# Layer norms of a decoder trunk, run in two halves of the tokens between dense products

## The chip, the cores and the metric

One core of a Trainium2 chip runs the whole program once. The metric is the device time of one launch in microseconds (us).

## What is computed

The program is one inference step of a decoder trunk: 512 prompt tokens and 8 sample tokens (520 columns) of width 1024 go through two layers. Each layer is a mixer and a gated ConvFFN, and a layer norm follows each of the four sublayers. The products are the bulk of it. Cut to what matters here:

```python
ALPHA = (2 * DEPTH) ** 0.25
def layer_norm(x, g, b):
    mu = jnp.mean(xf, axis=-1, keepdims=True)
    var = jnp.mean(jnp.square(xf - mu), axis=-1, keepdims=True)
    return ((xf - mu) * lax.rsqrt(var + NORM_EPS) * g + b)
def run_trunk(...):
    for layer in range(DEPTH):
        h = mixer(x)                 # gla/retention in layer 0, short convolution in layer 1
        x = layer_norm(ALPHA * x + h, ln1_g[layer], ln1_b[layer])
        h = conv_ffn(x, ...)         # (silu(g) * a) @ w_out after x @ w_in and a width-3 convolution
        x = layer_norm(ALPHA * x + h, ln2_g[layer], ln2_b[layer])
```

## The kernel before

Activations lie with features on the partitions: x32 is 8 feature tiles (KD = 8) of 128 x 520. Every dense product is done with both operands split into a high and a low part (x_hi, x_lo, w_hi, w_lo), so one 128-feature step is three matmuls, and the 520 tokens are two halves of 256 and 264 columns (HALVES), one PSUM bank each. Weights come in units of 1024 x 256 (the FFN's output product: three units of 8, 8 and 6 feature steps for 256 outputs). A unit makes two output tiles, f = 0 and 1, in acc(0) and acc(1), and costs 96 matmuls (72 where it has 6 steps). For each unit SyncE loads w_raw, ScalarE copies it to w_hi (stage_hi, L317), VectorE subtracts to w_lo (stage_lo, L322); the next unit's w_hi waits until the unit two before it has been used.

There is no scheduler: every engine's order is written out by hand, and semaphores tie them. There are four layer norms, n = 0 to 3. Norm 0 follows the mixer's output product, norm 1 the first FFN's, norm 2 the short convolution's, and norm 3 ends the program. At each of norms 0 to 2 this happens. The last weight unit of the output product makes feature tiles 6 and 7. VectorE adds each finished tile to x32 (L1480) and to a running sum ln_s1 (L1487); ScalarE squares it (L1110); GpSimd adds the squares up in ln_s2 (L901). Then TensorE sums over the partitions: token_sums (L687) is five matmuls with a single column of ones, for ln_s2, ln_s1 and the last square. VectorE turns these into mean and variance (L1511 to L1517), ScalarE takes the root (L1131), and TensorE spreads mean and inverse deviation over the partitions (spread, L696). VectorE adds the mean (L1534) and multiplies by the inverse (L1538), tile by tile; ScalarE applies gain and bias (L1148) and copies to x_hi (L1149); GpSimd makes x_lo (L859). The next product's first unit (first_unit and k_step, L356 and L359) consumes x_hi and x_lo tile by tile as they come. These float32 matmuls of sums and spreads leave two records each in the trace. Tile 5's handling on VectorE has the sums of tiles 0 to 5 in it (L1489, L1487), followed by stage_lo of the next product's first unit.

After the first unit of an FFN, accumulator acc(0) is free again only when ScalarE (L1166, L1168) and then VectorE (L1554, L1555, L1558) have read it; the second unit begins in acc(0). After norm 1 the short convolution's product follows, and one ScalarE copy (L1196) frees acc(0).

## Time and profile before

| | us |
|---|---|
| median of 3 runs | 1405.11 |
| lowest, highest | 1399.22, 1409.91 |
| span of the profiled execution | 1409.5 |
| PE busy in it | 1362.5 (97%) |
| DVE, ACT, POOL busy | 711.2, 482.1, 113.4 |
| mean granted TensorE clock | 0.956 |

The span is the hardware profiler's time from the first to the last instruction of one execution. It lies 0.4 us under the highest of the three runs and 4.4 us above their median; no time apart from the span is given for the profiled execution. TensorE is busy 97% of the span, so the kernel ends when TensorE has worked through its list. A granted clock of 1.00 is 2.4 GHz, of 0.50 it is 1.2 GHz.

### The profile page before, as it was taken

What the parts mean: (1) busy time and instruction counts of PE and PEld (TensorE: products, weight loads), DVE (VectorE), ACT (ScalarE), POOL (GpSimd) and SP (SyncE); (2) the same over time, 40 slices, a digit from 0 to 9 for tenths busy, and PEclk for the clock granted to TensorE, in tenths of its full rate; (3) what the DMA queues carried; (4) which work ended last, traced back from release to release, by engine and by line L of the source; (5) the groups of instructions that cost most, each with busy time, mean ns of one, the idle gap of its engine ahead of it and who ended that gap; (6) DMA issues with size and microseconds to landing.
All of it is one profiled execution on the core that took longest, in us unless ns stands there. A gap on an engine that the chain in (4) does not pass through costs nothing.

```text
span 1409.5 us, 24966 instructions
## 1 busy us (share of the span) xinstructions
PE 1362.5 (97%) x10861; PEld 1336.9 (95%) x10861; DVE 711.2 (50%) x905; ACT 482.1 (34%) x640; POOL 113.4 (8%) x77
## 2 busy tenths in 40 slices
PE   7999999999999999999999899999999999999994
PEld 6899998899989999999999899999899999999994
DVE  2657832234666565654225443346656656552255
ACT  3433231132354343443122433323543434341232
POOL 3000003100230000000002300002300000000023
PEclk9999998698989999999999899999899999999996
DMA  7222212311212222223222122222123222233201
GB/s 252 84 69 90 64 61 82 120 46 47 74 61 89 90 89 89 90 89 112 83 90 83 61 90 89 90 90 92 61 73 106 88 91 89 89 98 119 97 23 61
DMA packets 123556, 121.91 MB, mean 86 GB/s; under 512 B 2481, under 2 KB 121164, under 8 KB 123476
## 3 DMA queue, kind: packets, MB, share of 16 engines
q1 hardware_dynamic: 112916, 115.32, 25.2%
q10 hardware_dynamic: 10432, 5.24, 1.3%
q8 instruction: 52, 0.85, 0.2%
q0 software_dynamic: 144, 0.39, 0.1%
q14 instruction: 12, 0.10, 0.0%
HBM read 114.79 MB, written 6.55 MB: 86 GB/s over the span
## 4 chain that ended last, share of the span: by engine, by line
PE 89%; DVE 4%; ACT 2%; SPq 1%; POOL 1%; DMA 1%; issue 1%; DVEq 0%; ACTq 0%; POOLq 0%
PE ps L344 26%; PE ps L346 25%; PE ps L345 25%; PE ps L687 2%; PE ps L542 2%; PE ps L356 1%; PE ps L696 1%; POOL x_lo L859 1%; ACT x L1148 1%; PE ps L675 1%; ACT x_hi L1149 1%; DMA w_raw<-in_w_mix_in 1%; PE ps L359 1%; DVE tmp L1487 1%; DVE y_tok L1526 1%; SPq L404 1%
## 5 line engine op out<-in xcount | busy, mean ns | idle before, releaser
L344 PE MATMUL ps<-x_hi,w_hi 128*128 128x256 f32 (+1 forms) x2144 | 616.9, 288 | 0.0
L346 PE MATMUL ps<-x_hi,w_lo 128*128 128x256 f32 (+1 forms) x2144 | 611.0, 285 | 0.0
L345 PE MATMUL ps<-x_lo,w_hi 128*128 128x256 f32 (+1 forms) x2144 | 609.2, 284 | 0.0
L344 PEld LDWEIGHTS ps<-x_hi,w_hi 128*128 128x128 f32 x2144 | 409.9, 191 | 2.7 <-issue 1.2
L345 PEld LDWEIGHTS ps<-x_lo,w_hi 128*128 128x128 f32 x2144 | 411.0, 192 | 0.1
L346 PEld LDWEIGHTS ps<-x_hi,w_lo 128*128 128x128 f32 x2144 | 409.9, 191 | 0.0
L322 DVE TENSOR_TENSOR w_lo<-w_raw,w_hi 128x2048 fp32r<-128x2048 f32 (+2 forms) x103 | 234.9, 2280 | 238.1 <-ACT w_hi L317 237.8
L317 ACT ACTIVATE w_hi<-w_raw 128x2048 fp32r<-128x2048 f32 (+2 forms) x103 | 192.6, 1870 | 188.1 <-PE ps L346 174.7
L344 PE MATMUL ps<-h_hi,w_hi 128*128 128x264 f32 (+1 forms) x896 | 254.7, 284 | 0.8 <-DVE x L1491 0.8
L346 PE MATMUL ps<-h_hi,w_lo 128*128 128x264 f32 (+1 forms) x896 | 252.7, 282 | 0.0
L345 PE MATMUL ps<-h_lo,w_hi 128*128 128x264 f32 (+1 forms) x896 | 252.7, 282 | 0.0
L344 PEld LDWEIGHTS ps<-h_hi,w_hi 128*128 128x128 f32 x896 | 168.3, 188 | 1.1 <-DVE w_lo L322 1.0
L346 PEld LDWEIGHTS ps<-h_hi,w_lo 128*128 128x128 f32 x896 | 168.8, 188 | 0.0
L345 PEld LDWEIGHTS ps<-h_lo,w_hi 128*128 128x128 f32 x896 | 168.7, 188 | 0.1
L1166 ACT ACTIVATE tmp<-ps,vecs 128x520 f32<-128x520 f32 x88 | 69.2, 786 | 174.6 <-PE ps L346 166.3
L901 POOL TENSOR_TENSOR tmp<-tmp 128x520 f32<-128x520 f32 x24 | 34.4, 1435 | 1010.8 <-ACT tmp L1110 1009.8
L1554 DVE TENSOR_TENSOR tmp<-tmp,past_ffn 128x8 f32<-128x8 f32 x88 | 15.2, 173 | 128.9 <-ACT last_rows L1168 128.9
L1558 DVE SCALAR_TENSOR_TENSOR tmp<-ps,vecs,tmp 128x510 f32<-128x510 f32 x88 | 65.9, 749 | 11.2 <-DVE tmp L1555 1.5
L1555 DVE SCALAR_TENSOR_TENSOR tmp<-ps,vecs,tmp 128x511 f32<-128x511 f32 x88 | 65.9, 749 | 0.0
L1173 ACT ACTIVATE tmp<-tmp 128x520 f32<-128x520 f32 x44 | 28.1, 639 | 84.2 <-DVE tmp L1558 84.2
L859 POOL TENSOR_TENSOR x_lo<-x,x_hi 128x520 fp32r<-128x520 f32 x32 | 47.9, 1511 | 45.3 <-ACT x_hi L1149 34.2
L1565 DVE TENSOR_TENSOR h_lo<-tmp,h_hi 128x520 f32 (+1 forms) x44 | 30.8, 700 | 40.1 <-ACT h_hi L1175 40.1
(233 smaller groups left out, 1124.6 us busy)
## 6 DMA issues: line engine op xcount, KB each, us to landing
w_raw<-in_w_ffn_in SPq DMA_DIRECT2D x44, 1024.0 KB, 4.9
w_raw<-in_w_ffn_out SPq DMA_DIRECT2D x16, 1024.0 KB, 5.0
w_raw<-in_w_mix_in SPq DMA_DIRECT2D x14, 1024.0 KB, 5.1
w_raw<-in_w_sc_in SPq DMA_DIRECT2D x12, 1024.0 KB, 4.9
w_raw<-in_w_ffn_out SPq DMA_DIRECT2D x8, 768.0 KB, 4.5
w_raw<-in_w_mix_out SPq DMA_DIRECT2D x4, 1024.0 KB, 5.1
w_raw<-in_w_sc_out SPq DMA_DIRECT2D x4, 1024.0 KB, 5.2
x_tok<-in_x_prompt SPq DMA_DIRECT2D x2, 1024.0 KB, 7.6
```

The costliest lines, as they stand in the source:

```text
L317: e.activation(w_hi[:, par, 0:k, 0:c], w_raw[:, par, 0:k, 0:c], ACT.Copy).then_inc(hi_made, 1)
L322: e.tensor_tensor(w_lo[:, par, 0:k, 0:c], w_raw[:, par, 0:k, 0:c], w_hi[:, par, 0:k, 0:c].bitcast(F32), ALU.subtract).then_inc(lo_made, 1)
L344: e.matmul(out, wh, xh[:, k, lo:hi], start=(first and i == 0), stop=False)
L345: e.matmul(out, wh, xl[:, k, lo:hi], start=False, stop=False)
L346: mm = e.matmul(out, wl, xh[:, k, lo:hi], start=False, stop=(last and i == len(ks) - 1))
L542: mm = e.matmul(bank(4 + h, P, c * C, C), k[p, h // 2, t], q[p, h // 2, t], start=True, stop=True)
L859: e.tensor_tensor(x_lo[:, f, :], x32[:, f, :], x_hi[:, f, :].bitcast(F32), ALU.subtract).then_inc(sem("x_made"), 1)
L901: e.tensor_tensor(ln_s2, ln_sq[:, 0, :] if t == 1 else ln_s2, ln_sq[:, t % 4, :], ALU.add).then_inc(sem("ln_added"), 1)
L1166: e.activation(tmp[:, 2 * s + f, :], acc(f), ACT.Identity, bias=ffn_vec(l, 3, tile), scale=ffn_vec(l, 2, tile))
L1555: e.scalar_tensor_tensor(t[:, 1:T], acc(f)[:, 0:T - 1], ffn_vec(l, 1, tile), t[:, 1:T], ALU.mult, ALU.add).then_inc(sem("tap_done"), 1)
L1558: e.scalar_tensor_tensor(t[:, 2:T], acc(f)[:, 0:T - 2], ffn_vec(l, 0, tile), t[:, 2:T], ALU.mult, ALU.add).then_inc(acc_free, 1)
L1565: e.tensor_tensor(h_lo[:, bass.ds(2 * i + f, 1), :], tmp[:, 6 + f:7 + f, :], h_hi[:, bass.ds(2 * i + f, 1), :].bitcast(F32), ALU.subtract) ...
```

## The change

Norms 0, 1 and 2 are worked in the two halves of the tokens. The last unit of the output product (closing_unit) does both tiles of tokens 0 to 255 first, then both tiles of tokens 256 to 519. The sums of the first half of the tokens stand in the middle of its third quarter, the two spreads of that half in its fourth quarter. The first unit of the next product (opening_unit) does tokens 0 to 255 of all 8 feature steps first, with the second half's sums ahead of step 2, and its spreads ahead of steps 4 and 5; then it does tokens 256 to 519. VectorE, ScalarE and GpSimd do the adds, squares, shifts, scalings and splits in halves too, in a new order. The gain goes from ScalarE into VectorE's scaling. Norm 3 keeps its order. The core of the diff:

```diff
+        TOKEN_TILES = [(0, 1), (2, 3, 4)]
+        TILES, ADDED = KD + 2, KD - 1
...
-            def token_sums(out, squares, start=True, stop=True):
-                for j in range(5):
+            def token_sums(out, squares, start=True, stop=True, js=range(5)):
+                for j in js:
...
             def ln_sums(n):
...
-                e.wait_ge(sem("ln_mean_made"), n + 1)
-                spread(2, ln_inv[:, 1, :]).then_inc(sem("ln_spread"), 1)
-                e.wait_ge(sem("ln_inverse"), n + 1)
-                spread(3, ln_inv[:, 0, :]).then_inc(sem("ln_spread"), 1)
...
+            def half_sums(n, half):
+
+                js = TOKEN_TILES[half]
+                e.wait_ge(sem("ln_added"), ADDED * n + 6 + half)
+                token_sums(bank(7, P, 0, 5), ln_s2, True, False, js)
+                e.wait_ge(sem("ln_totaled"), TILES * n + 8 + 2 * half)
+                token_sums(bank(5, P, 0, 5), ln_s1, js=js).then_inc(sem("ln_var"), 1)
+                e.wait_ge(sem("ln_squared"), TILES * n + 8 + 2 * half)
+                token_sums(bank(7, P, 0, 5), ln_sq[:, (KD - 1) % 4, :], False, js=js).then_inc(sem("ln_var"), 1)
+
+            def half_mean(n, half):
+                e.wait_ge(sem("ln_mean_made"), 2 * n + half + 1)
+                spread(2, ln_inv[:, 1, :], TOKEN_TILES[half]).then_inc(sem("ln_spread"), 1)
+
+            def half_scale(n, half):
+                e.wait_ge(sem("ln_inverse"), 2 * n + half + 1)
+                spread(3, ln_inv[:, 0, :], TOKEN_TILES[half]).then_inc(sem("ln_spread"), 1)
...
+            def closing_unit(n, pr, u, k0, ks, only, xh, xl):
+
+
+                e.wait_ge(lo_made, u + 1)
+                for half in range(2):
+                    for f in range(2):
+                        if only and not half:
+                            e.wait_ge(acc_free, 2 * pr + f - 1)
+                        for i in range(ks):
+                            if half and f == 0 and i == ks // 2:
+                                half_sums(n, 0)
+                            if half and f == 1 and i == 0:
+                                half_mean(n, 0)
+                            if half and f == 1 and i == 2:
+                                half_scale(n, 0)
+                            mm = half_k(u % 2, i, f, k0 + i, half, xh, xl, only and i == 0, i == ks - 1)
...
+            def opening_unit(n, u, pr):
+
+
+                made = KD + 2 * KD * n
+                e.wait_ge(lo_made, u + 1)
+                e.wait_ge(sem("ln_centered"), TILES * n + 8)
+                for half in range(2):
+                    if half:
+                        e.wait_ge(acc_free, 2 * pr)
+                    both = [(k, f) for k in range(KD if half == 0 else KD // 2) for f in range(2)]
+                    apart = [(k, f) for f in range(2) for k in range(KD // 2, KD)] if half else []
+                    for k, f in both + apart:
+                        if half == 0 and f == 0:
+                            if k == 2:
+                                half_sums(n, 1)
+                            if k == 4:
+                                half_mean(n, 1)
+                            if k == 5:
+                                half_scale(n, 1)
+                        lo, hi = HALVES[half]
+                        wh, wl = (w[:, u % 2, k, f * P:(f + 1) * P] for w in (w_hi, w_lo))
+                        e.wait_ge(sem("x_hi_made"), made + KD * half + k + 1)
+                        e.matmul(acc_half(f, half), wh, x_hi[:, k, lo:hi], start=(k == 0), stop=False)
+                        e.matmul(acc_half(f, half), wl, x_hi[:, k, lo:hi], start=False, stop=False)
+                        e.wait_ge(sem("x_made"), made + KD * half + k + 1)
+                        mm = e.matmul(acc_half(f, half), wh, x_lo[:, k, lo:hi], start=False, stop=(k == KD - 1))
...
+                for half, (lo, hi) in enumerate(HALVES):
+                    e.wait_ge(sem("ln_squared"), TILES * n + 7 + 2 * half)
+                    e.tensor_tensor(ln_s2[:, lo:hi], ln_s2[:, lo:hi], ln_sq[:, 2, lo:hi], ALU.add).then_inc(sem("ln_added"), 1)
+                for half, (lo, hi) in enumerate(HALVES):
+                    for f in range(KD):
+                        split_x(f, KD + 2 * KD * n + KD * half + f + 1, lo, hi)
...
+                def half_x(f, half):
+                    lo, hi = HALVES[half]
+                    e.wait_ge(sem("ln_scaled"), 2 * KD * n + KD * half + f + 1)
+                    link(e.activation(x32[:, f, lo:hi], x32[:, f, lo:hi], ACT.Identity, bias=vec(g, col_b + f)))
+                    e.activation(x_hi[:, f, lo:hi], x32[:, f, lo:hi], ACT.Copy).then_inc(sem("x_hi_made"), 1)
...
+                half_square(6, 0)
+                half_square(7, 0)
+                half_root(0)
+                half_square(6, 1)
                 for f in range(KD):
-                    e.wait_ge(sem("ln_scaled"), KD * n + f + 1)
-                    link(e.activation(x32[:, f, :], x32[:, f, :], ACT.Identity, bias=vec(g, col_b + f), scale=vec(g, col_g + f)))
-                    e.activation(x_hi[:, f, :], x32[:, f, :], ACT.Copy).then_inc(sem("x_hi_made"), 1)
+                    if f == 2:
+                        half_square(7, 1)
+                    half_x(f, 0)
+                half_root(1)
+                stage_hi(e, u + 4 * per + 1)
+                for f in range(KD):
+                    half_x(f, 1)
...
                     for g in range(per):
                         stage_lo(e, u + per * j + g + 1)
+                    if j == 3 and n < 2 * DEPTH - 1:
+                        break
...
+                def scaled(half):
+                    lo, hi = HALVES[half]
+                    made = 2 * KD * n + KD * half
+                    for f in range(KD + 2):
+                        if half == 0 and f == 4:
+                            closing(1, 1)
+                        if f < KD:
+                            e.wait_ge(sem("ln_spread"), 4 * n + 2 * half + 1)
+                            e.tensor_tensor(x32[:, f, lo:hi], x32[:, f, lo:hi], acc_half(2, half), ALU.add).then_inc(sem("ln_shifted"), 1)
+                        if f >= 2:
+                            e.wait_ge(sem("ln_spread"), 4 * n + 2 * half + 2)
+                            e.wait_ge(sem("ln_shifted"), made + f - 1)
+                            e.scalar_tensor_tensor(x32[:, f - 2, lo:hi], x32[:, f - 2, lo:hi], vec(V_LN, col_g + f - 2), acc_half(3, half),
+                                                   ALU.mult, ALU.mult).then_inc(sem("ln_scaled"), 1)
+
+                closing(0, 0)
+                closing(1, 0)
+                moments(0)
+                closing(0, 1)
+                scaled(0)
+                moments(1)
+                scaled(1)
+                stage_lo(e, NEXT[n] + 1)
```

TensorE at norm 0 before, from the last dense products of the output product to the first of the FFN (ones,tmp are the token sums, ident,ln_inv the spreads):

```order
L344 MATMUL ps<-h_hi,w_hi 128x264
L345 MATMUL ps<-h_lo,w_hi 128x264
L346 MATMUL ps<-h_hi,w_lo 128x264
L687 MATMUL ps<-ones,tmp 128x1 x15
L696 MATMUL ps<-ident,ln_inv 128x128 x4
L696 MATMUL ps<-ident,ln_inv 128x8
L696 MATMUL ps<-ident,ln_inv 128x128 x4
L696 MATMUL ps<-ident,ln_inv 128x8
L356 MATMUL ps<-x_hi,w_hi 128x256
L356 MATMUL ps<-x_hi,w_hi 128x264
```

TensorE at norm 0 now: the first half's sums inside the closing unit, whose dense products go on behind them:

```order
L803 MATMUL ps<-h_hi,w_hi 128x264
L804 MATMUL ps<-h_hi,w_lo 128x264
L805 MATMUL ps<-h_lo,w_hi 128x264
L689 MATMUL ps<-ones,tmp 128x1 x6
L803 MATMUL ps<-h_hi,w_hi 128x264
L804 MATMUL ps<-h_hi,w_lo 128x264
L805 MATMUL ps<-h_lo,w_hi 128x264
```

and the second half's sums, ahead of feature step 2 of the opening unit:

```order
L850 MATMUL ps<-x_hi,w_hi 128x256
L851 MATMUL ps<-x_hi,w_lo 128x256
L853 MATMUL ps<-x_lo,w_hi 128x256
L689 MATMUL ps<-ones,tmp 128x1 x9
L850 MATMUL ps<-x_hi,w_hi 128x256
L851 MATMUL ps<-x_hi,w_lo 128x256
L853 MATMUL ps<-x_lo,w_hi 128x256
```

Where 15 sums and two whole spreads stood in one block between two products, there are now blocks of 6 and 9 sums, and dense products stand behind each.

VectorE at norm 0 before, from the running sums of tiles 0 to 5 (tmp) over stage_lo (w_lo) to tiles 6 and 7 and the mean:

```order
L1489 COPY tmp<-x_49 128x520
L1487 TENSOR_TENSOR tmp<-tmp,x_49 128x520 x5
L322 TENSOR_TENSOR w_lo<-w_raw,w_hi 128x2048
L1480 TENSOR_TENSOR x_49<-x_49,ps 128x520
L1482 MEMSET ones_one 128x1
L1487 TENSOR_TENSOR tmp<-tmp,x_49 128x520
L1480 TENSOR_TENSOR x_49<-x_49,ps 128x520
L1482 MEMSET ones_one 128x1
L1487 TENSOR_TENSOR tmp<-tmp,x_49 128x520
L1511 TENSOR_SCALAR ln_inv<-ps 128x5
```

and now, the same stretch:

```order
L1594 COPY tmp<-x_49 128x520
L1592 TENSOR_TENSOR tmp<-tmp,x_49 128x520 x5
L324 TENSOR_TENSOR w_lo<-w_raw,w_hi 128x2048
L1621 TENSOR_TENSOR x_49<-x_49,ps 128x256
L1626 TENSOR_TENSOR tmp<-tmp,x_49 128x256
L1621 TENSOR_TENSOR x_49<-x_49,ps 128x256
L1626 TENSOR_TENSOR tmp<-tmp,x_49 128x256
L1632 TENSOR_SCALAR ln_inv<-ps 128x2
L1634 TENSOR_TENSOR ln_var<-ln_inv 128x2
L1636 SCALAR_TENSOR_TENSOR ln_var<-ps,ln_var 128x2
L1638 RECIPROCAL ln_inv<-ln_inv 128x2
L1621 TENSOR_TENSOR x_49<-x_49,ps 128x264
```

The running sums and stage_lo stand where they stood; behind them come four half operations, on which the first half's sums wait, and the first half's mean and inverse come before the second half of tile 6.

ScalarE at norm 1 before, from the last squares (tmp) over stage_hi of the next product's second unit (w_hi) and the root to the first outputs:

```order
L1110 ACTIVATE tmp<-x_49 128x520 x3
L317 ACTIVATE w_hi<-w_raw 128x2048
L1131 ACTIVATE ln_inv<-ln_var,eps 128x5
L1148 ACTIVATE x_49<-x_49,vecs 128x520
L1149 ACTIVATE x_hi<-x_49 128x520
L1148 ACTIVATE x_49<-x_49,vecs 128x520
L1149 ACTIVATE x_hi<-x_49 128x520
L1148 ACTIVATE x_49<-x_49,vecs 128x520
L1149 ACTIVATE x_hi<-x_49 128x520
```

and now, at the passage from the first half's outputs to the second half's:

```order
L1209 ACTIVATE x_49<-x_49,vecs 128x256
L1210 ACTIVATE x_hi<-x_49 128x256
L1209 ACTIVATE x_49<-x_49,vecs 128x256
L1210 ACTIVATE x_hi<-x_49 128x256
L1204 ACTIVATE ln_inv<-ln_var,eps 128x3
L319 ACTIVATE w_hi<-w_raw 128x2048
L1209 ACTIVATE x_49<-x_49,vecs 128x264
L1210 ACTIVATE x_hi<-x_49 128x264
L1209 ACTIVATE x_49<-x_49,vecs 128x264
L1210 ACTIVATE x_hi<-x_49 128x264
```

stage_hi of the second unit stood ahead of the root, and now stands behind the first half's outputs and ahead of the second half's; so it does at norms 0 and 2.

## Rows read from the trace of the kernel before

**Rows 1.** The page, part 1: busy us, share of the span, instructions.

```profile
PE 1362.5 (97%) x10861; PEld 1336.9 (95%) x10861; DVE 711.2 (50%) x905; ACT 482.1 (34%) x640; POOL 113.4 (8%) x77
```

**Rows 2.** Timeline of TensorE at norm 0: start, us, then idle before.

```profile
369.62 0.28 PE L344 MATMUL ps<-h_hi,w_hi 128*128 128x256 f32 x1
...
380.99 0.28 PE L346 MATMUL ps<-h_hi,w_lo 128*128 128x264 f32 x1
381.67 3.88 PE L687 MATMUL ps<-ones,tmp 128*128 128x1 f32 x30 [0.40 <-POOL tmp L901]
385.41 4.41 PE L696 MATMUL ps<-ident,ln_inv 128*128 128x128 f32 x20
392.23 0.77 PE L356 MATMUL ps<-x_hi,w_hi 128*128 128x256 f32 x2 [2.40 <-ACT x_hi L1149]
...
408.12 0.36 PE L344 MATMUL ps<-x_hi,w_hi 128*128 128x256 f32 x1
```

**Rows 3.** The same at norm 1.

```profile
769.67 0.28 PE L344 MATMUL ps<-h_hi,w_hi 128*128 128x256 f32 x1
...
778.17 0.28 PE L346 MATMUL ps<-h_hi,w_lo 128*128 128x264 f32 x1
...
790.26 0.48 PE L356 MATMUL ps<-x_hi,w_hi 128*128 128x256 f32 x2 [2.40 <-ACT x_hi L1149]
...
806.12 0.28 PE L344 MATMUL ps<-x_hi,w_hi 128*128 128x256 f32 x1
```

**Rows 4.** Windows at norms 0 and 1: us, PE busy (x), granted clock, DMA.

```profile
384.50:385.00 0.50, 0.50 (x6) 0.67 0.00 0
...
398.00:398.50 0.50, 0.50 (x4) 0.68 0.00 0
...
780.50:781.00 0.50, 0.50 (x5) 0.61 0.00 0
...
797.50:798.00 0.50, 0.50 (x6) 0.82 0.00 0
```

**Rows 5.** Chain that ended last, merged: sums and spreads amid dense work.

```profile
291.64 4.36 PE ps L687 x40
300.45 2.13 PE ps L696 x20
```

**Rows 6.** Timeline of VectorE at norm 0, then at norm 1.

```profile
376.61 2.28 DVE L322 TENSOR_TENSOR w_lo<-w_raw,w_hi 128x2048 fp32r<-128x2048 f32 x1
...
774.18 0.70 DVE L1480 TENSOR_TENSOR x<-x,ps 128x520 f32<-128x520 f32 x1
```

**Rows 7.** Timeline of ScalarE at norm 0.

```profile
382.58 1.89 ACT L317 ACTIVATE w_hi<-w_raw 128x2048 fp32r<-128x2048 f32 x1
...
390.60 0.82 ACT L1148 ACTIVATE x<-x,vecs 128x520 f32<-128x520 f32 x1 [4.44 <-DVE x L1538]
391.45 0.64 ACT L1149 ACTIVATE x_hi<-x 128x520 fp32r<-128x520 f32 x1
391.99 0.81 ACT L1148 ACTIVATE x<-x,vecs 128x520 f32<-128x520 f32 x1
...
405.47 0.79 ACT L1166 ACTIVATE tmp<-ps,vecs 128x520 f32<-128x520 f32 x1 [2.20 <-PE ps L359]
```

**Rows 8.** Timelines of VectorE and GpSimd at norm 0, where the two meet.

```profile
397.75 3.38 DVE L322 TENSOR_TENSOR w_lo<-w_raw,w_hi 128x2048 fp32r<-128x2048 f32 x1
...
399.07 3.23 POOL L859 TENSOR_TENSOR x_lo<-x,x_hi 128x520 fp32r<-128x520 f32 x1
...
402.26 1.30 POOL L859 TENSOR_TENSOR x_lo<-x,x_hi 128x520 fp32r<-128x520 f32 x1
```

**Rows 9.** Groups by line and form: shapes xcount, then busy us, mean ns.

```profile
L981 ACT ACTIVATE k_tok<-ps 128x256 f32<-128x256 f32 x4 | 1.2, 389 | 0.3 <-PE ps L557 0.3
L945 ACT ACTIVATE gate_t<-ps,vecs 128x520 f32<-128x520 f32 x2 | 1.3, 692 | 1.4 <-PE ps L524 1.4
...
L1399 DVE SCALAR_TENSOR_TENSOR samp<-samp,a_samp,ps 128x128 f32<-128x128 f32 x16 | 4.3, 340 | 4.0 <-PE ps L662 4.0
```

178 lines of the change are left out of this document (106 added, 72 removed).

## The prediction

> **What bounds the kernel now.** The page's busy times come first: TensorE is busy 97% of the span [rows 1], so the end moves only with TensorE's list, its waits and its clock. The timeline of TensorE at a norm shows what the change can reach [rows 2, 3]. At norm 0 the closing unit starts at 369.62 and its last dense product ends at 381.27 (380.99 + 0.28): 96 matmuls in 11.65 us, 0.121 each. The next product's second unit begins at 408.12. Between lie 26.85 us, of which the first unit's 96 matmuls need 11.65, so norm 0 costs 15.2 us. At norm 1 the same reading gives 806.12 - 778.45 = 27.7 and a cost of 16.0. Norm 2 repeats norm 0. Together 46.4 us.
>
> Three things are in it. First, work: 30 records of sums and 20 of spreads [rows 2]; amid dense work these took 4.36 / 40 = 0.109 and 2.13 / 20 = 0.107 us each [rows 5], so 3.3 + 2.1 = 5.4 us. Second, waiting: 2.40 us for the first x_hi [rows 2, 3], and small gaps. Third, the clock: it fell to the 1.2 GHz level in the window at 384.50, three us after the dense products stopped, and came back in the window at 398.00, six us after they resumed at 392.23; at norm 1 it fell in the window at 780.50 and returned in the one at 797.50 [rows 4, 2, 3].
>
> **The work stays, so at most 30 us can go.** Sums and spreads are the same in number (6 + 9 and 4 + 6 against 15 and 10). If nothing else were left, norms 0 and 2 would gain 15.2 - 5.4 = 9.8 each and norm 1 10.6: 30.2 us. What is left has to be followed along three engines.
>
> **Half operations.** The trace has few of 256 columns. On ScalarE a copy of 256 columns takes 0.39 from PSUM [rows 9], and a copy of 520 takes 0.64 from SBUF [rows 7]; I take 0.42 for the half copy (bounds 0.32, half of the long one, and 0.64), as the 0.39 row is the nearest. Identity with a bias alone takes 0.69 at 520 [rows 9] against 0.82 with bias and gain [rows 7]; half of it with the same fixed part, 0.52 (bounds 0.35 and 0.69). A half tile therefore costs ScalarE about 0.97 from scaled x to x_hi, and one follows another every 0.87. VectorE: 0.34 at 128 columns [rows 9] and 0.70 at 520 [rows 6] give 0.46 at 256 (bounds 0.35 and 0.70). GpSimd: 1.30 at 520 [rows 8]; half 0.65, and I take 0.70 (bounds 0.65 and 1.30).
>
> **Norm 0, closing unit.** TensorE reaches the first half's sums after 48 + 12 matmuls, at 369.62 + 7.3 = 376.9. They wait for tiles 6 and 7 of that half on VectorE. VectorE is not there: its running sums end at 376.61 and its stage_lo runs until 378.9 [rows 6], and both stand ahead of the half operations as before. Before, that lag was covered by the second tile's dense products, which ended at 381.27. Now four half operations (1.7 us, the pairs overlapping a little) end at 380.6, and **a new stall of 3.7 us** stands in the middle of the closing unit. Six sums follow (12 records, 1.3 us), then 36 dense matmuls (4.4) and four spreads (0.9; mean and inverse are ready by then, since the root's chain is under 1 us). At full clock the unit ends at 387.2.
>
> The clock won't stay full. From 376.9 to 381.9 no dense product runs, longer than the 2.1 to 3.4 us after which it fell in the two cases above, and it then took six us of work to return. I take half rate from 380.6 to about 388: 7.4 us in which half the work is done, a loss of 3.7, and the closing unit ends at 390.9. The Trainium skill (TensorE: Matmul & The Clock Gate, "HAM oscillation — how this bites in real kernels") says that short runs of matmuls broken by waits keep throwing the clock back, which speaks against this change; the trace agrees in the windows named.
>
> **Norm 0, opening unit.** Now ScalarE is the pace. VectorE adds the second half of tile 7 first (0.95, to 391.9), then shifts tile 4 and scales tile 2 (0.8, to 392.7). ScalarE makes tile 2 (393.7) and five more at 0.87 (398.0). Then come root (0.3) and the second unit's stage_hi (1.9 [rows 7]), which before was done at 384.5 under TensorE's sums and now stands between the halves: 400.2. The second half's tiles follow: 401.1 for the first, seven more at 0.88 for the last, 407.3. GpSimd's last split ends at 408.0, and tile f = 0 is complete at 408.1. The dense work, sums and spreads of the opening unit fit beneath this as long as the clock is full. The second unit can't start yet: acc(0) must be read first. Before, ScalarE began that at 405.47 [rows 7] and the second unit started at 408.12, 2.65 us later, just covered by f = 1's products. Now f = 1 has only 12 matmuls left behind f = 0 (1.45 us), so 1.2 us of it come into the open. Start at 410.8 against 408.12: **+2.7**.
>
> One more price. When stage_lo and GpSimd's split met, the first took 3.38 in place of 2.28 and the second 3.23 in place of 1.30 [rows 8, 6]: one waited for the other. Behind scaled(1) the second unit's stage_lo now meets the last splits of the second half. If GpSimd is held for 1.6 to 1.9 us there, the start becomes 412.4, or +4.3. The Trainium skill (SBUF — State Buffer, "SBUF: two separate sides") has a rule for it: a VectorE operation with two SBUF inputs and a GpSimd one that reads SBUF exclude each other for the whole instruction. By it the sum would be +4.3 for each such norm, without it +2.7; rows 8 agree with the rule.
>
> I take **+3.5 for norms 0 and 2 each**. The lower bound is the chain without the loss of clock, 2.7 - 3.7 = -1.0, the upper one +5.5 (the lock, and the clock falling once more at the second half's nine sums, 1.9 us of work in which no dense product runs).
>
> **Norm 1.** Here the output product has three units for a pair of tiles, and VectorE is free at 774.18 [rows 6]. TensorE gets to the sums after 36 + 9 matmuls, at 769.67 + 5.4 = 775.1; the half operations end at 775.9, a stall of 0.8. The closing unit ends at 781.4, tile 2 of x_hi is made at 784.1, the first half at 788.4, stage_hi at 790.6, the second half at 797.7, x_lo at 798.4. A ScalarE copy frees acc(0), so the second unit follows f = 1's products, at 800.0 against 806.12: -6.1. The meeting of stage_lo and GpSimd takes 1.8 back, one fall of the clock in the opening unit about as much again. I take **-2.5**; bounds -6.1 and +1.
>
> **The sum.** 2 x 3.5 - 2.5 = +4.5 us. Against the profiled span it gives 1409.5 + 4.5 = 1414.0. That span lies 4.4 above the median of the three runs, so I add the term to the median: 1405.1 + 4.5 = **1409.6**. With all lower bounds it is -8.1 (1397), with all upper ones +12 (1417). The rest of the program is untouched.
>
> **Rivals.** *The halves hide the norm (faster by over 1%).* If VectorE got through tile 6 and 7 in time and the clock never fell, the 30.2 us above would go: 1375. It counts as faster from -14 us on, which needs norms 0 and 2 to gain 4 each. For it: the waits of today [rows 2, 3] do vanish, and norm 1 has VectorE free. Against it: the lag of VectorE in rows 6 and stage_hi between the halves. Chance 0.12.
>
> *The clock stays low through both units (slower by over 1%).* Mechanism: the stall in the closing unit drops it, the second half's nine sums and the waits for x_hi in the opening unit keep it low. From 390.9, 96 matmuls at 0.242 (23.2), nine sums (3.9) and six spreads (2.6) end at 420.6, +12.5 at norms 0 and 2; at norm 1 the same 29.7 us from 781.4 give +5. Total +30: 1435. It counts as slower from +14, when it holds for about half of that. For it: at norm 0 the clock was low for 13.5 us in a row [rows 4]. Against it: it came back amid products that were fed tile by tile. Chance 0.12.
>
> *The change doesn't shorten or lengthen anything,* because the halves end up in the old order: the order of instructions shows that they don't. Chance 0.02, within 1%.
>
> **Chances and range.** A measurement of this kernel can't tell 1% (14 us) from no change, as its three runs lie 10.7 us apart. My forecast (-8 to +12) has 0.74. Faster 0.12, within 1% 0.76, slower 0.12. The range from 1393 to 1421 takes in the bounds, the scatter of the runs, and a part of either rival.
>
> **What would show it.** In the changed kernel's timeline of TensorE: a gap of 3 to 4 us before the first half's sums at norms 0 and 2, and under 1 us at norm 1; half clock behind it for six us or more; the opening unit's steps spaced 0.87; no dense product in the last us before the second unit of an FFN. On ScalarE, w_hi between the two halves of x_hi. I am wrong if the gap is missing (VectorE's order or durations misread), if the half operations cost far more than interpolated (GpSimd's at 1.3 would add up to 5 us a norm), or if the clock holds through the gap.

## The result, and the profile after

The changed kernel takes 1415.9 us (median of 9 runs, 1408.18 to 1418.94), the kernel before 1408.73 (9 runs in the same comparison). The ratio is 1.0071, 95% interval 1.0052 to 1.009: slower by 0.7%, inside the 1% that the prediction calls no change, and inside its range (1393 to 1421). The interval lies clear of 1, so nine runs do tell 0.7% from nothing, though the prediction held that a measurement could not tell 1%. The profiled spans are 1417.1 and 1409.5.

A **passage** below is the time from the closing unit's first matmul to the first matmul of the next product's second unit. It holds all that the change touches. In each profiled run on record the time lies 1.8 us above the span. So the changed kernel's profile is the longest of its nine runs (1418.94, 3.0 above the median), and that of the kernel before would be a time of about 1411.3, 2.6 above its median: their difference stands, but the sum of the passages of either may be up to 3 us long for its kernel. The profiles of the other runs below lie between 2.8 us under (e9) and 4.3 us over (e10) their medians.

| passage, us | norm 0 | norm 1 | norm 2 | sum |
|---|---|---|---|---|
| before [rows 2, 3] | 38.50 | 36.45 | 38.44 | 113.39 |
| after | 43.18 | 36.64 | 42.42 | 122.24 |

The three passages grew by 8.85 us and the spans by 7.6, so the whole loss lies in them (the stretch ahead of norm 0, which is untouched, was 1.3 shorter). The page, part 1, in the form of rows 1:

```profile
PE 1364.7 (96%) x10861; PEld 1336.9 (94%) x10861; DVE 720.2 (51%) x977; ACT 491.6 (35%) x697; POOL 118.8 (8%) x104
```

TensorE has the same matmuls and only 2.2 us more busy time; the rest is waiting. Its timeline at norm 0 (start, us, idle before) answers to rows 2:

```profile
368.31 0.28 PE L803 MATMUL ps<-h_hi,w_hi 128*128 128x256 f32 x1
...
379.33 2.17 PE L689 MATMUL ps<-ones,tmp 128*128 128x1 f32 x12 [3.72 <-POOL tmp L984]
...
390.96 2.06 PE L689 MATMUL ps<-ones,tmp 128*128 128x1 f32 x18
...
406.03 0.39 PE L853 MATMUL ps<-x_lo,w_hi 128*128 128x264 f32 x1 [1.86 <-POOL x_lo L934]
...
411.49 0.36 PE L346 MATMUL ps<-x_hi,w_hi 128*128 128x256 f32 x1 [0.37 <-DVE tmp L1702]
```

and at norm 1 to rows 3:

```profile
779.63 1.50 PE L689 MATMUL ps<-ones,tmp 128*128 128x1 f32 x12 [1.08 <-POOL tmp L984]
...
785.80 0.36 PE L850 MATMUL ps<-x_hi,w_hi 128*128 128x256 f32 x1 [0.38 <-ACT x_hi L1210]
...
804.53 0.39 PE L853 MATMUL ps<-x_lo,w_hi 128*128 128x264 f32 x1 [1.88 <-POOL x_lo L934]
```

Two waits stand out: 3.72 us before the first half's sums at norm 0 (3.61 at norm 2, 1.08 at norm 1), and 1.85 to 1.88 for an x_lo at all three norms. The x_lo waited for is that of feature step 4 of the second half, the first of the four steps in which the opening unit finishes f = 0 before it starts f = 1. VectorE at norm 0 shows where the first comes from, as rows 6 did before: w_lo still stands ahead of the four half operations.

```profile
375.34 2.29 DVE L324 TENSOR_TENSOR w_lo<-w_raw,w_hi 128x2048 fp32r<-128x2048 f32 x1
377.54 0.41 DVE L1621 TENSOR_TENSOR x<-x,ps 128x256 f32<-128x256 f32 x1
377.99 0.42 DVE L1626 TENSOR_TENSOR tmp<-tmp,x 128x256 f32<-128x256 f32 x1
...
403.09 2.29 DVE L324 TENSOR_TENSOR w_lo<-w_raw,w_hi 128x2048 fp32r<-128x2048 f32 x1
```

GpSimd's split beside the last of these rows, the meeting of rows 8 again:

```profile
403.22 2.76 POOL L934 TENSOR_TENSOR x_lo<-x,x_hi 128x264 fp32r<-128x264 f32 x1
```

This split of 264 columns is recorded at 2.76 us, beside w_lo from 403.09 to 405.38; the splits behind it take 0.75. This time w_lo started first, and GpSimd was held and not VectorE.

The clock by windows (us, PE busy, PEld, DVE, ACT, POOL busy, granted clock, DMA) answers to rows 4:

```profile
379.50:380.00 0.50, 0.50 (x6) 0.50 (x6) 0.06 (x1) 0.00 (x0) 0.00 (x0) 0.96 1.05 373
...
386.50:387.00 0.50, 0.50 (x6) 0.50 (x5) 0.00 (x0) 0.00 (x0) 0.00 (x0) 0.71 0.00 0
...
393.50:394.00 0.50, 0.50 (x5) 0.50 (x4) 0.50 (x3) 0.47 (x3) 0.50 (x1) 0.61 0.00 0
...
397.00:397.50 0.50, 0.50 (x6) 0.50 (x5) 0.50 (x2) 0.50 (x1) 0.40 (x1) 0.97 0.00 0
...
407.00:407.50 0.50, 0.42 (x4) 0.21 (x3) 0.00 (x0) 0.23 (x2) 0.50 (x2) 0.77 0.80 254
...
410.50:411.00 0.50, 0.50 (x4) 0.41 (x3) 0.46 (x2) 0.00 (x0) 0.00 (x0) 0.82 0.00 0
```

At norm 0 it falls three times, behind the 3.72 us wait, behind the second half's sums and behind the x_lo wait, and is low for some 13.6 us in all (6.8 + 3.4 + 3.4), as long as before. ScalarE at norm 0, where rows 7 were; its groups by line (xcount, then busy us, mean ns, idle before) and, in the second fence, its timeline between the halves:

```profile
L1209 ACT ACTIVATE x<-x,vecs 128x256 f32<-128x256 f32 (+1 forms) x16 | 8.0, 500 | 3.7 <-DVE x L1652 3.5
L1210 ACT ACTIVATE x_hi<-x 128x256 fp32r<-128x256 f32 (+1 forms) x16 | 6.7, 421 | 0.5
```

```profile
396.49 0.29 ACT L1204 ACTIVATE ln_inv<-ln_var,eps 128x3 f32<-128x3 f32 x1
396.68 1.90 ACT L319 ACTIVATE w_hi<-w_raw 128x2048 fp32r<-128x2048 f32 x1
398.71 0.52 ACT L1209 ACTIVATE x<-x,vecs 128x264 f32<-128x264 f32 x1
...
408.84 0.78 ACT L1269 ACTIVATE tmp<-ps,vecs 128x520 f32<-128x520 f32 x1 [1.59 <-PE ps L853]
```

Sixteen half tiles cost 8.0 + 6.7 = 14.7 us of ScalarE; the eight whole ones cost 6.5 + 5.1 = 11.6. So the change adds 3.1 us to ScalarE's row at every norm. Halving alone adds 3.9, since the gain's move takes 0.8 off (e7: eight whole tiles without the gain cost 5.7 + 5.1 = 10.8). The last row is the first reading of acc(0): it starts at 408.84, and the second unit follows at 411.49, 2.65 us later, as before.

### The profile page after: what moved, and what is told of

Its sections match the earlier page's. It is cut to its first block, busy times and chain, and to the rows that moved or that the text cites. A ratio compares the mean times of both kernels' runs of the same rounds, so it can differ in the third digit from the quotient of the medians.

```text
span 1417.1 us, 25164 instructions
## 1 busy us (share of the span) xinstructions
PE 1364.7 (96%) x10861; PEld 1336.9 (94%) x10861; DVE 720.2 (51%) x977; ACT 491.6 (35%) x697; POOL 118.8 (8%) x104
## 4 chain that ended last, share of the span: by engine, by line
PE 89%; DVE 3%; ACT 2%; SPq 1%; POOL 1%; issue 1%; DMA 1%; ACTq 0%; DVEq 0%; POOLq 0%
PE ps L346 26%; PE ps L348 25%; PE ps L347 25%; PE ps L689 2%; PE ps L544 2%; PE ps L698 1%; PE ps L358 1%; POOL x_lo L934 1%; PE ps L677 1%; DMA w_raw<-in_w_mix_in 1%; DVE y_tok L1680 1%; DVE tmp L1592 1%; SPq L406 1%; ACT x L1209 1%; ACT x_hi L1210 1%
## 5 line engine op out<-in xcount | busy, mean ns | idle before, releaser
L324 DVE TENSOR_TENSOR w_lo<-w_raw,w_hi 128x2048 fp32r<-128x2048 f32 (+2 forms) x103 | 231.6, 2249 | 236.6 <-ACT w_hi L319 236.3
L346 PE MATMUL ps<-h_hi,w_hi 128*128 128x264 f32 (+1 forms) x808 | 229.8, 284 | 0.8 <-DVE x L1596 0.8
L347 PE MATMUL ps<-h_lo,w_hi 128*128 128x264 f32 (+1 forms) x808 | 228.0, 282 | 0.0
L348 PE MATMUL ps<-h_hi,w_lo 128*128 128x264 f32 (+1 forms) x808 | 227.9, 282 | 0.0
L346 PEld LDWEIGHTS ps<-h_hi,w_hi 128*128 128x128 f32 x808 | 151.8, 188 | 1.2 <-DVE w_lo L324 1.0
L347 PEld LDWEIGHTS ps<-h_lo,w_hi 128*128 128x128 f32 x808 | 152.1, 188 | 0.1
L348 PEld LDWEIGHTS ps<-h_hi,w_lo 128*128 128x128 f32 x808 | 152.2, 188 | 0.0
L977 POOL TENSOR_TENSOR tmp<-tmp 128x520 f32<-128x520 f32 x21 | 30.9, 1473 | 998.0 <-ACT tmp L1193 997.1
L1702 DVE SCALAR_TENSOR_TENSOR tmp<-ps,vecs,tmp 128x510 f32<-128x510 f32 x88 | 65.9, 749 | 11.2 <-DVE tmp L1699 1.5
L934 POOL TENSOR_TENSOR x_lo<-x,x_hi 128x256 fp32r<-128x256 f32 (+2 forms) x56 | 52.4, 946 | 34.0 <-ACT x_hi L1210 20.6
```

What stands on the lines that cost most here:

```text
L324: e.tensor_tensor(w_lo[:, par, 0:k, 0:c], w_raw[:, par, 0:k, 0:c], w_hi[:, par, 0:k, 0:c].bitcast(F32), ALU.subtract).then_inc(lo_made, 1)
L346: e.matmul(out, wh, xh[:, k, lo:hi], start=(first and i == 0), stop=False)
L347: e.matmul(out, wh, xl[:, k, lo:hi], start=False, stop=False)
L348: mm = e.matmul(out, wl, xh[:, k, lo:hi], start=False, stop=(last and i == len(ks) - 1))
L934: e.tensor_tensor(x_lo[:, f, lo:hi], x32[:, f, lo:hi], x_hi[:, f, lo:hi].bitcast(F32), ALU.subtract).then_inc(sem("x_made"), 1)
L977: e.tensor_tensor(ln_s2, ln_sq[:, 0, :] if t == 1 else ln_s2, ln_sq[:, t % 4, :], ALU.add).then_inc(sem("ln_added"), 1)
```

## The experiments

Each kernel is the changed one with the edit shown, save e7, which is the kernel before with one part of the change. Passages come from one profiled execution each; ratios are to the kernel before, from its runs of the same batch.

| run | norm 0 | norm 1 | norm 2 | sum | ratio [95% interval] |
|---|---|---|---|---|---|
| after | 43.18 | 36.64 | 42.42 | 122.24 | 1.0071 [1.0052, 1.009] |
| e1 w_lo late | 39.28 | 33.67 | 38.05 | 111.00 | 1.0017 [0.9995, 1.0039] |
| e2 filled | 39.94 | 36.24 | 40.33 | 116.51 | 1.0043 [1.0023, 1.0063] |
| e3 apart | 43.28 | 32.81 | 42.12 | 118.21 | 1.0069 [1.0042, 1.0097] |
| e4 w_hi early | 43.49 | 36.49 | 42.61 | 122.59 | 1.0092 [1.0064, 1.012] |
| e6 root early | 43.19 | 36.63 | 42.46 | 122.28 | one run, 1418.44 us |
| e8 pairs | 44.12 | 34.34 | 43.74 | 122.20 | 1.0109 [1.0072, 1.0146] |
| e5 combined | 39.35 | 32.40 | 39.05 | 110.80 | 1.0007 [0.999, 1.0023] |
| e7 gain alone | 38.99 | 34.46 | 37.39 | 110.84 | 1.0006 [0.9989, 1.0023] |
| e9 no fill | 37.96 | 34.75 | 39.23 | 111.94 | 1.0004 [0.9983, 1.0026] |
| e10 fill | 37.97 | 36.33 | 38.10 | 112.40 | 0.9996 [0.9976, 1.0016] |
| e11 no bias | 35.97 | 31.11 | 36.07 | 103.15 | 0.9982 [0.9951, 1.0014] |

**e1: w_lo behind the first half's moments.** VectorE's order alone: the first unit's stage_lo stands behind the first half's mean and inverse.

```diff
                 moments(0)
+                stage_lo(e, u + 4 * per)
                 closing(0, 1)
```

(and the same stage_lo is taken out of the loop ahead of the closing unit)

> The changed kernel, with VectorE's stage_lo of the next product's first unit moved from ahead of the half operations on tiles 6 and 7 to behind the first half's mean and inverse. A passage is the time from the closing unit's first matmul to the first matmul of the next product's second unit; the passages at norms 0, 1, 2 took 43.2, 36.6, 42.4 us in the changed kernel and 38.5, 36.5, 38.4 in the kernel before. Theory 1 (VectorE's lag makes the stall, and the stall drops the clock): the stall before the first half's sums shrinks from 3.7 to about 1.5 us at norms 0 and 2, the clock holds through the closing unit, passages of 38 to 40 us there and little change at norm 1; 4 to 8 us less than the changed kernel in all. Rival (the halves themselves cost it, by more and shorter operations): the passages shrink by at most 1 us each.

Measured: the sum of the passages fell by 11.2 and the timed ratio by 0.0054, which is 7.6 us. Of the gap between the two, 3.0 may be that the changed kernel's profile was that much above its median. The kernel can no longer be told from the one before. TensorE's wait at norm 0, then its clock in two windows:

```profile
376.84 1.39 PE L689 MATMUL ps<-ones,tmp 128*128 128x1 f32 x11 [1.50 <-POOL tmp L984]
```

```profile
378.00:380.00 2.00, 2.00 (x13) 2.00 (x13) 1.45 (x5) 0.30 (x1) 0.00 (x0) 0.64 0.01 4
380.00:382.00 2.00, 2.00 (x12) 2.00 (x11) 1.96 (x4) 0.30 (x1) 0.00 (x0) 0.51 0.00 0
```

2.2 us of the wait are gone and the passage lost 3.9, so the wait cost more than itself: the clock is back in the window at 382 in place of 386.5. The x_lo waits of 1.84 to 1.87 stayed. Two parts of the expectation failed. The clock did not hold through the closing unit at norm 0 (at norm 2 it did), and norm 1 got 3.0 us shorter where little was expected: its wait of 1.08 is gone, and its clock is low for 3.4 us instead of 10. VectorE's lag is the largest single cost of the change.

**e2: dense products in the place of the wait.** Thirty products into an accumulator half that is not used then, at norms 0 and 2; their result is thrown away.

```diff
                             if half and f == 0 and i == ks // 2:
+                                for _ in range(30 if n in (0, 2) else 0):
+                                    e.matmul(acc_half(3, 0), w_hi[:, u % 2, 0, 0:P], xh[:, k0, 0:HA], start=True, stop=True)
                                 half_sums(n, 0)
```

> The changed kernel, with 30 added dense matmuls of 256 columns into an unused accumulator ahead of the first half's sums at norms 0 and 2, where TensorE stands still for 3.7 us (30 at 0.12 make 3.6 us). They are work that no output needs. Theory 1's second half (the fall of the clock costs as much as the stall itself): the clock stays at 2.4 GHz through the closing unit, and each of the two passages gets about 3 us shorter, 43.2 to 40 and 42.4 to 40, though TensorE does more. Rival (the clock's loss is covered, since ScalarE sets the pace): the passages stay within 1 us.

Measured: 3.2 and 2.1 us less at norms 0 and 2, 0.4 at norm 1, which has no filling. The sums start as late after the closing unit's start (11.02 us, as in the changed kernel); only the clock differs, full behind them:

```profile
379.42 1.28 PE L689 MATMUL ps<-ones,tmp 128*128 128x1 f32 x10 [0.17 <-POOL tmp L986]
```

```profile
380.00:382.00 2.00, 2.00 (x19) 2.00 (x19) 0.65 (x4) 0.30 (x1) 0.00 (x0) 1.00 1.07 379
```

Later falls changed with it: at norm 0 the one behind the second half's sums is gone too (the clock is low for 3.4 us of the passage, 13.6 in the changed kernel), at norm 2 one more came in the opening unit (6.8 us against 10.2). So 2 to 3 us a norm is what the fall in the closing unit costs with what follows from it.

**e3: the second unit's w_lo waits for the last split.**

```diff
                 scaled(1)
+                e.wait_ge(sem("x_made"), KD + 2 * KD * (n + 1))
                 stage_lo(e, NEXT[n] + 1)
```

> The changed kernel, with VectorE waiting for the last of GpSimd's splits before the second unit's stage_lo, so that the two never run together there. Theory 2 (they exclude each other, and the 1.9 us gap of TensorE on x_lo comes from it): the 2.76 us split becomes 0.75, the gap of 1.9 us goes at all three norms, and the fall of the clock behind it with it; passages 2 to 3.5 us shorter each, at norm 1 34 us. Rival (the split is long for another reason, or stage_lo becomes late and TensorE waits for it): the passages stay as they are, or grow by up to 2 us.

Measured: the x_lo wait falls from 1.86 to 0.23 at all three norms, and norm 1 gains 3.8. Part of the 3.8 is the clock, which is low there for 3.4 us instead of some 10. Norms 0 and 2 gain nothing. TensorE, VectorE and ScalarE at norm 0:

```profile
409.57 0.55 PE L346 MATMUL ps<-x_hi,w_hi 128*128 128x256 f32 x1 [3.14 <-DVE tmp L1703]
```

```profile
404.57 2.29 DVE L324 TENSOR_TENSOR w_lo<-w_raw,w_hi 128x2048 fp32r<-128x2048 f32 x1 [3.42 <-POOL x_lo L934]
...
408.68 0.75 DVE L1703 SCALAR_TENSOR_TENSOR tmp<-ps,vecs,tmp 128x510 f32<-128x510 f32 x1
```

```profile
406.92 0.78 ACT L1269 ACTIVATE tmp<-ps,vecs 128x520 f32<-128x520 f32 x1 [1.70 <-DVE ones_one L1728]
```

There TensorE finishes f = 1 early and waits 3.14 for acc(0) to be read. But this very edit makes the reading late: ScalarE waits 1.70 us for a memset that stands on VectorE just behind the w_lo that was held back (404.57 to 406.86). The rival's second half (stage_lo becomes late) came true in this form. So e3 shows what the meeting does to the split (2.76 becomes 0.75), and not what norms 0 and 2 would gain without it: if the reading had begun when ScalarE was free for it behind f = 0, at 405.2, and had taken the 2.65 us from there to the second unit, the second unit would start at 407.9 instead of 409.57. This is an estimate; no run shows it.

**e4: w_hi inside the first half's row.**

```diff
                     if f == 2:
                         half_square(7, 1)
+                        stage_hi(e, u + 4 * per + 1)
                     half_x(f, 0)
                 half_root(1)
-                stage_hi(e, u + 4 * per + 1)
```

> The changed kernel, with ScalarE's stage_hi of the second unit moved from between the two halves of x_hi to the place where ScalarE waits for tile 2 of the first half (idle 1.1 to 1.4 us there). Theory 3 (it delays the second half by its full 1.9 us): the first half's later tiles come about 0.8 us later, the second half's about 1.1 us earlier, and each passage is about 1 us shorter. Rival (it delays the first half on the path): no change, or up to 1 us longer, above all at norm 1, where ScalarE was idle for less.

Measured: no gain (122.59 against 122.24). ScalarE at norm 0:

```profile
400.67 0.28 ACT L1204 ACTIVATE ln_inv<-ln_var,eps 128x3 f32<-128x3 f32 x1
402.63 0.52 ACT L1209 ACTIVATE x<-x,vecs 128x264 f32<-128x264 f32 x1 [1.68 <-DVE x L1652]
```

Without w_hi behind the root ScalarE is idle for 1.68 us, since inverse, spread and scaling follow the root in a chain. The second half's row starts 30.7 us after the closing unit's start, against 30.4 in the changed kernel. w_hi had stood in the shadow of that chain, and the theory that it delays the second half by its full 1.9 us falls.

**e6: the root earlier.** half_root(1) stands ahead of half_x(6, 0) instead of behind half_x(7, 0).

> The changed kernel with only the second half's root moved ahead of tile 6 of the first half on ScalarE. It asks why moving stage_hi out of the passage from first to second half brought nothing: there ScalarE stood idle 1.7 us for the first scaled tile of the second half, since root, inverse, spread and scaling follow one another. Theory 4 (that chain, not stage_hi, sets the second half's start): with the root 1.4 us earlier the second half's first x_hi comes earlier only as far as stage_hi lets it, so here 0 to 0.5 us a passage. Rival (stage_hi sets it after all): 0, and the run that moved stage_hi would then have gained.

Measured: 122.28, the same. The root comes 1.4 us earlier after the closing unit's start (26.8 against 28.2), but w_hi is still between the halves, and the second half's row starts at 30.5 us, as before. Both of its theories allowed for no change, so this run does not choose between them. e4 and e6 together show two bounds of nearly the same length side by side, the chain from the root and w_hi: either one alone keeps the second half where it is. What taking away both would bring was not run.

**e8: the opening unit's second half in pairs.** Feature steps 4 to 7 go f = 0, f = 1 in turn, as steps 0 to 3 do.

```diff
-                    both = [(k, f) for k in range(KD if half == 0 else KD // 2) for f in range(2)]
-                    apart = [(k, f) for f in range(2) for k in range(KD // 2, KD)] if half else []
+                    both = [(k, f) for k in range(KD) for f in range(2)]
+                    apart = []
```

> The changed kernel, with the second half of the opening unit in pairs of tiles to the end (f = 0 and 1 at every feature step) instead of f = 0's last four steps ahead of f = 1's. f = 0 then ends one matmul triple before f = 1. My term in question: behind an FFN's first unit the second one waits for acc(0) to be read (2.65 us after f = 0), so f = 1's 12 matmuls are free there; at norm 1 the reading takes 0.65 us and they are not. By it: norms 0 and 2 within 0.5 us, norm 1 shorter by about 0.8 us. Rival (TensorE's own work behind f = 0 sets the start everywhere): all three shorter by 0.8 to 1 us.

Measured: norm 1 gains 2.3, of which part is the clock again (low for 6.8 us instead of some 10), norms 0 and 2 lose 0.9 and 1.3 (within 0.5 was expected), with this wait at norm 0:

```profile
405.60 0.36 PE L346 MATMUL ps<-x_hi,w_hi 128*128 128x256 f32 x1 [2.08 <-DVE tmp L1702]
```

The wait is 0.37 in the changed kernel, and at norm 2 it goes from 0.71 to 2.38. Doing f = 0 first helps where acc(0) has long readers and costs where one copy frees it.

**e5: three parts together.** e1, e6, and e3's wait at norm 1 alone.

> The changed kernel with three edits: the first unit's stage_lo behind the first half's mean and inverse on VectorE (as in the run that did this alone: passages 39.3, 33.7, 38.1 us), at norm 1 only the second unit's stage_lo behind the last split (alone it took norm 1 from 36.6 to 32.8), and the second half's root on ScalarE ahead of tile 6 of the first half. Passages in the kernel before: 38.5, 36.5, 38.4, sum 113.4. Theory 1 with the exclusion of VectorE and GpSimd: the gains add up, 38.5, 30, 37.5, sum about 106, and the time is 5 to 8 us under the kernel before (ratio 0.995). Rival (the shorter lag only lets the next limit show, and gains don't add): sum near 110, ratio 0.998 to 1.0.

Measured: 110.80, against 111.00 for e1 by itself. Norm 1 gained 1.3 in place of 3.8, and its second unit then waits 0.49 for the w_lo that e3's wait holds back. The rival (gains don't add) came true.

**e7: the gain alone.** The kernel before, whole tiles; VectorE's multiplication takes the gain in, and ScalarE's Identity loses its scale.

```diff
-                        e.tensor_tensor(x32[:, f - 2, :], x32[:, f - 2, :], acc(3), ALU.mult).then_inc(sem("ln_scaled"), 1)
+                        e.scalar_tensor_tensor(x32[:, f - 2, :], x32[:, f - 2, :], vec(V_LN, col), acc(3), ALU.mult, ALU.mult
+                                               ).then_inc(sem("ln_scaled"), 1)
```

> The kernel before, with one part of the change alone: the gain goes from ScalarE's operation into VectorE's scaling at norms 0 to 2, with no halves. ScalarE's 0.81 us per tile becomes about 0.73, VectorE's 0.69 becomes 0.75. In the kernel before ScalarE paces the opening unit with 1.385 us a tile, so 8 tiles give 0.6 us a passage: sum of the passages 113.4 to about 111.6, ratio 0.999, which timing can't tell from 1. Rival (the operation with a per-partition factor is slower on the path or meets GpSimd): passages grow.

Measured: Identity falls from 809 to 717 ns and the passages by 2.6 in the one profile, but the timed ratio is 1.0006. On whole tiles the gain's move neither made nor hid the loss by more than the timing can tell.

**e9 and e10: the moves together, without and with a little filling.** e1's move, and at norm 1 alone e3's wait and e8's pairs; e10 has 12 filling products at norms 0 and 2.

> The three moves that each shortened a passage, put together without the root's move: w_lo of the second unit behind the first half's moments (all norms); at norm 1 alone the wait for the last split ahead of the next w_lo, and tiles 4 to 7 of the opening unit's second half in pairs. Theory 'each removes its own wait': norms 0 and 2 stay as in the run with w_lo late (39.3 and 38.1), norm 1 falls from 33.7 by 3.8 for the lock and 2.3 for the pairs, to 28 to 30; sum of the passages 106 to 107, against 113.4 before: 6 to 7 us, a ratio of 0.995 to 0.997. Rival 'they cover one another': at norm 1 ScalarE's row of half tiles is next, which the combined run showed at 32.4; then the sum stays at 110 and the ratio at 1.000.

> The same with 12 dense products of 256 columns, whose result is not used, ahead of the first half's sums at norms 0 and 2 (12 x 0.107 = 1.3 us, about the wait that is left there with w_lo late, 1.50 and 1.41). Theory 'the wait lets the clock fall': the wait shrinks to 0.2 to 0.3, the fall at 380 comes later or not at all, and each of the two passages gets 1 to 3 us shorter: sum 102 to 105, ratio 0.992 to 0.995. Rival 'the sums themselves let it fall': six sums and four spreads of one column or 128 are enough, the windows at 380 to 386 stay at 0.50, and norms 0 and 2 change by less than 0.5 us each.

Measured: both equal to the kernel before within 0.3%; the sums are 111.94 and 112.40, where 106 to 107 and 102 to 105 were expected. (The stage_lo moved behind the moments is that of the first unit, as in e1; the text above calls it the second's.)

At norm 1 the pairs bring nothing on top, because TensorE then waits for the w_lo that the wait for the last split holds back. VectorE and TensorE of e9 there:

```profile
795.02 2.29 DVE L324 TENSOR_TENSOR w_lo<-w_raw,w_hi 128x2048 fp32r<-128x2048 f32 x1 [3.42 <-POOL x_lo L935]
```

```profile
797.36 0.39 PE L346 MATMUL ps<-x_hi,w_hi 128*128 128x256 f32 x1 [1.57 <-DVE w_lo L324]
```

The filling can be judged by all passages with e1's order at norms 0 and 2. Six have no filling and a wait of 1.41 to 1.54 us (e1, e5, e9). In four of them the clock fell behind the wait, and they took 39.05 to 39.35; in two it held (e9 at norm 0, e1 at norm 2), and they took 37.96 and 38.05. With the filling, which leaves a wait under 0.1, it held at both norms of e10 (37.97 and 38.10). So it is the wait that lets the clock fall there, and not the sums by themselves, which run at full clock in e10; the fall costs 1.0 to 1.4 us with what follows from it, and where the clock holds anyway the filling changes nothing. In e10 the clock is full at norm 0 from 374 to 408:

```profile
384.00:386.00 2.00, 1.08 (x8) 0.72 (x6) 1.96 (x7) 1.47 (x4) 0.50 (x1) 1.00 1.05 367
...
390.00:392.00 2.00, 2.00 (x20) 2.00 (x19) 0.90 (x4) 1.94 (x5) 1.76 (x3) 1.00 0.00 0
```

Still the passage is 37.97, and 37.96 in e9. So neither this wait nor the clock is what is left: between 388 and 402 ScalarE is busy for 1.92 to 1.97 us of every 2. The code of norm 1 is the same in both, and its passages are 34.75 and 36.33: the clock is low for 6.8 us in e9 and for 10.2 in e10.

**e11: ScalarE's row made short.** e10 without the norm's bias: the Identity operation is left out, so the values behind each norm lack it.

```diff
-                    link(e.activation(x32[:, f, lo:hi], x32[:, f, lo:hi], ACT.Identity, bias=vec(g, col_b + f)))
```

> The same as the run with 12 filling products, with one thing left out of the computation: ScalarE does not add the norm's bias to the half tiles (no Identity operation), so a half tile costs it one copy (0.42) in place of Identity and copy (a step of 0.86). Theory 'with the clock held, the row of half tiles on ScalarE sets the passage': the first half's tiles come at VectorE's step, 0.73, in place of 0.86, for 16 tiles 2 us less, and root follows a half tile sooner; norms 0 and 2 fall from 38.0 and 38.1 to 35 to 36, norm 1 by as much, sum of the passages 103 to 107 against 112.4, ratio 0.994 to 0.997. Rival 'GpSimd's splits and its lock with w_lo are as late': GpSimd takes 0.75 for each half split, the last ones still stand behind w_lo, and the passages change by less than 0.7 each; ratio 0.999 to 1.001.

Measured: against e10 every passage fell, by 2.0, 5.2 and 2.0. Norms 0 and 2 came to 35.97 and 36.07, where 35 to 36 was expected, with the clock as in e10. ScalarE at norm 0 now waits for VectorE:

```profile
L1212 ACT ACTIVATE x_hi<-x 128x256 fp32r<-128x256 f32 (+1 forms) x16 | 6.6, 421 | 5.8 <-DVE x L1655 5.8
```

TensorE waits at the same two places:

```profile
400.74 0.39 PE L856 MATMUL ps<-x_lo,w_hi 128*128 128x264 f32 x1 [2.11 <-POOL x_lo L937]
...
404.59 0.36 PE L346 MATMUL ps<-x_hi,w_hi 128*128 128x256 f32 x1 [1.29 <-DVE tmp L1708]
```

So ScalarE's row of sixteen pairs set part of the passage. At norm 1 part of the 5.2 is the clock, which is low for 3.4 us here, 6.8 in e9 and 10.2 in e10 (against e9 the passage fell by 3.6). The timing is weaker than the profile: 0.9982, with 1 inside its interval. That ScalarE's row is a bound rests on the profile; that its removal pays in time is not shown.

## Why the prediction was right, and where it was off

Predicted 1409.6, +4.5 on the kernel before. Measured 1415.9 against 1408.73, +7.2 by the medians, +7.6 by the profiles. Of the 6.3 us between forecast and time, 3.6 is the starting value, the median of three runs (1405.11) where that of nine is 1408.73, and 2.7 is the effect. The sign, the outcome within 1% and the mechanisms were right; the terms were too small, norm 1 most.

**The stall before the first half's sums** was put at 3.7 us and is 3.72 [rows 6 gave it]; norm 1 was put at 0.8 and is 1.08. e1 shows that VectorE's order is its cause.

**The clock in the closing unit** was put at half rate from 380.6 to 388 for 3.7 us. It fell in the window at 379.5 and was back in that at 386.5; e2 gives 2.1 to 3.2 for it with what follows from it. The closing unit ended at 389.36, predicted 390.9 from a start 1.3 us later: a match.

**The half operations** were 0.42 (ScalarE copy, predicted 0.42), 0.50 (Identity, 0.52), 0.41 to 0.49 (VectorE, 0.46) and 0.72 to 0.75 (GpSimd, 0.70). The step of 0.87 came out as 0.86 [rows 7 against the group above].

**Norms 0 and 2, +3.5 each**, came out at +4.7 and +4.0. The working had +2.7 from the chain and +4.3 with GpSimd held by stage_lo, and I took a value between. The hold came in full at all three norms (1.86, 1.88, 1.85), so +4.3 was the value to take; the rule cited from the Trainium skill (SBUF — State Buffer, "SBUF: two separate sides") gave the same, and the trace agrees with it here: the split that took 2.76 us started behind w_lo and beside it. The rest of the chain came out as written: the last split ended 39.8 us after the closing unit's start, where the working with the hold has 40.0, and the second unit followed the first reading of acc(0) by the 2.65 us. The other bound of the term, a further fall of the clock at the second half's sums, came true at norm 0 too (0.61 in the window at 393.5), and so did a third one behind the x_lo wait, which I had not seen. By the passages with e1's order a fall in the closing unit costs 1.0 to 1.4 us.

**"stage_hi between the halves"** was wrong as a reason. I had it delay the second half by 1.9 us; e4 shows that it fills a wait of 1.7 in the chain from root to scaled tile. The time predicted there was right all the same (the second half's row starts 30.4 us after the closing unit's start, predicted 30.6), since the chain costs as much: that is luck, two bounds of the same length.

**Norm 1, -2.5**, came out at +0.2: this is the term that was mis-sized. The list had -6.1 from the chain, 1.8 back for the meeting and as much for one fall of the clock. Measured are two falls in the opening part (at 789.5 and 806.5) instead of one. They leave the clock low for 9.9 us of the passage, up to 4.9 us of work where 1.8 was put down. The first of them also breaks the claim that ScalarE paces the unit here, because TensorE reaches the second half's spreads late:

```profile
792.80 1.90 ACT L319 ACTIVATE w_hi<-w_raw 128x2048 fp32r<-128x2048 f32 x1
797.21 0.52 ACT L1209 ACTIVATE x<-x,vecs 128x264 f32<-128x264 f32 x1 [2.52 <-DVE x L1652]
```

ScalarE is done with w_hi at 794.7 and then stands still for 2.52 us for the second half's first scaled tile; VectorE's scaling in turn waited for the spread, which TensorE reached at 795.47, at half clock. The working had no wait there. Then TensorE comes out of the x_lo wait at 804.53 with 22 of the 24 products that are kept apart still to do, and reaches the second unit 5.15 us later. e3 (-3.8 without the meeting) and e8 (-2.3 without the separation) both shorten this, each with less of the clock's fall. How the 2.7 us divides between clock, meeting and separation is not shown. The gains don't add: with the meeting removed behind e1's move, e5 and e9 have 32.40 and 34.75 there against 33.67, and in both the second unit waits for the w_lo held back.

**The rivals.** *The halves hide the norm* needed VectorE ready in time and a full clock. e10 has nearly that at norms 0 and 2 and is still only equal to the kernel before: the working of this rival lacked ScalarE's row, 3.1 us longer in the new form, the meeting, and the reading of acc(0). *The clock stays low through both units* did not happen: inside the passages it came back three times at norm 0, once at norm 1 and twice at norm 2, as the reason against it said.

Of the 30.2 us ceiling nothing was won. At norm 0 a passage at full clock with no waits would be 38.50 - 15.2 + 5.4 = 28.7. Of the 14.5 us above that, e1's move takes 3.9, and the clock, where it held as well (e9), 1.3 more. Of the 9.3 that stay in e9, waits of 1.50 (first sums), 0.92 (first x_hi), 1.84 (the meeting) and 1.30 (acc(0)) make 5.6; the other 3.7 are small steps in which products come at the pace of the half tiles (e11, with a shorter row, has a passage 2.0 under e10's). I have not split these further, and no version tried beats the kernel before by more than its interval.

## What to carry to other kernels

Moving a reduction between dense products can pay only if the engines that feed it are as far ahead as TensorE will be: look in their timelines for what stands just ahead of the feeding operations, here a 2.3 us weight step that the old order covered. Splitting a tile in two costs the fixed part of each operation again (10.8 to 14.7 us on ScalarE here), which makes the pacing engine later while it makes the first result earlier. Where two bounds differ by whether a collision seen in the trace happens again, and the new order puts the same two operations side by side, take the bound with the collision. Before an edit that holds an operation back is read as a test, look at what stands behind that operation on its engine: in e3 and e9 the held w_lo became the next wait itself.
